# Recurrence of a two-layer encoder: diagonal blocks fetched by one DMA, level masks on VectorE, block inversion in one piece, four buffers of last decays

## What is computed

```python
def step(state, inp):
    r_t, w_t, k_t, v_t, kk_t, a_t = inp
    sk = jnp.einsum('bhij,bhj->bhi', state, kk_t)
    state = (state * w_t[:, :, None, :]
             - sk[..., None] * (kk_t * a_t)[:, :, None, :]
             + v_t[..., None] * k_t[:, :, None, :])
    y = jnp.einsum('bhij,bhj->bhi', state, r_t)
    return state, y
```

## Time and profile before

| | |
|---|---|
| median of 3 runs | 3150.53 us (3146.79 to 3151.83) |
| profiled execution: its own time | 3151.65 us |
| its span | 3149.8 us |
| busy PE / DVE / POOL / ACT | 86% / 54% / 41% / 30% of the span |
| recurrence, about 1627 to 2284 us | 657 us, a fifth of the span |
| in it PE / DVE / POOL / ACT busy | 431 / 432 / 257 / 150 us |
| mean granted clock of PE there | 0.84 |

### The profile page before, as it was taken

One profiled execution on the slowest core, in us unless ns is written; L12 is line 12 of the kernel. 1 busy time (PEld: TensorE's weight loads), 2 busy tenths in 40 slices (PEclk: granted clock), 3 DMA queues, 4 the chain that ended last, 5 costly groups with the idle time before them and its releaser, 6 DMA issues. The chain is left out here.

```text
span 3149.8 us, 48729 instructions
## 1 busy us (share of the span) xinstructions
PE 2694.7 (86%) x20064; PEld 2211.6 (70%) x20064; DVE 1692.8 (54%) x2038; ACT 930.1 (30%) x1543; POOL 1303.7 (41%) x662
## 2 busy tenths in 40 slices
PE   1887898999999999898965676777659999999999
PEld 1565676888877887776754566666647788878887
DVE  6745545665536344678635777777413543433444
ACT  2434433212233221545431222222124322222221
POOL 2532244444445343444433444444236444444443
PEclk9899998999999999999987988889879999999999
DMA  6421243545422232565752222222143233223333
GB/s 230 165 69 49 75 138 102 176 158 194 147 87 94 95 99 81 136 158 136 177 135 73 75 74 74 74 75 75 42 122 99 81 101 98 96 91 96 96 98 120
DMA packets 269146, 343.33 MB, mean 109 GB/s; under 512 B 180096, under 2 KB 180224, under 8 KB 268928
## 3 DMA queue, kind: packets, MB, share of 16 engines
q1 hardware_dynamic: 268928, 340.24, 35.8%
HBM read 298.29 MB, written 40.89 MB: 108 GB/s over the span
## 5 line engine op out<-in xcount | busy, mean ns | idle before, releaser
L687 POOL TENSOR_TENSOR wl<-w,wh 128x1024 fp32r<-128x1024 f32 x368 | 905.8, 2467 | 1308.5 <-ACT wh L728 1308.3
L180 PE MATMUL ps<-hi,wh 128*128 128x512 f32 x2208 | 883.1, 400 | 55.8 <-POOL wl L687 42.7
L181 PE MATMUL ps<-lo,wh 128*128 128x512 f32 x2208 | 868.9, 394 | 0.0
L182 PE MATMUL ps<-hi,wl 128*128 128x512 f32 x2208 | 868.8, 393 | 0.0
L728 ACT ACTIVATE wh<-w 128x1024 fp32r<-128x1024 f32 x368 | 388.1, 1057 | 717.6 <-DMA w<-in_ffn_w_in 529.7
L180 PEld LDWEIGHTS ps<-hi,wh 128*128 128x128 f32 x2208 | 420.3, 190 | 158.3 <-POOL wl L687 42.9
L994 DVE SCALAR_TENSOR_TENSOR xt<-ps,mod,xt 128x512 f32<-128x512 f32 x384 | 286.6, 750 | 438.3 <-PE ps L182 438.1
L181 PEld LDWEIGHTS ps<-lo,wh 128*128 128x128 f32 x2208 | 420.5, 190 | 89.9 <-issue 3.7
L182 PEld LDWEIGHTS ps<-hi,wl 128*128 128x128 f32 x2208 | 419.7, 190 | 90.1
L999 DVE TENSOR_TENSOR act<-ps,silu 128x512 f32<-128x512 f32 x88 | 60.8, 691 | 461.3 <-PE ps L182 461.3
L180 PE MATMUL ps<-act_hi,wh 128*128 128x512 f32 x704 | 282.8, 402 | 17.9 <-DVE act_lo L1003 10.9
(11 more groups left out here) (219 smaller groups left out, 3556.3 us busy)
## 6 DMA issues: line engine op xcount, KB each, us to landing
w<-in_ffn_w_in SPq DMA_DIRECT2D x176, 512.0 KB, 3.7
piece<-in_ada_w SPq DMA_DIRECT2D x96, 512.0 KB, 4.9
w<-in_ffn_w_out SPq DMA_DIRECT2D x88, 512.0 KB, 3.7
w<-in_w_rkv SPq DMA_DIRECT2D x48, 512.0 KB, 4.0
scratch<-silu SPq DMA_DIRECT2D x48, 256.0 KB, 3.1
scratch<-act SPq DMA_DIRECT2D x48, 256.0 KB, 3.0
w<-in_wqk SPq DMA_DIRECT2D x20, 512.0 KB, 4.6
xt<-in_xT SPq DMA_DIRECT2D x4, 2048.0 KB, 10.6
```

The lines of the kernel that those rows point to most:

```text
L180: pe.matmul(out, w_hi(k), x_hi(k), start=first and k == 0, stop=False)
L181: pe.matmul(out, w_hi(k), x_lo(k), start=False, stop=False)
L182: ins = pe.matmul(out, w_lo(k), x_hi(k), start=False, stop=last and k == kc - 1)
L687: pool.tensor_tensor(wl[n % NW][:, :, :], wr[n % NW][:, :, :], wh[n % NW][:, :, :].bitcast(F32), ALU.subtract).then_inc(*wlo.up)
```

## The change

Five edits, all in `wkv_phase`:

1. The images in memory are laid out by pair, half and row (each row of 64 numbers in a run of its own, 256 bytes), so that all 64 diagonal blocks can be addressed by one pattern. `n_diag` is read by one DMA instead of eight; `t_diag` and `t_diag_t` are written by one each instead of eight each. The transfers of whole images (N out, inverses in) keep their number; their runs become 256 bytes instead of 2 KB.
2. The two level masks are made by DVE from the gram in PSUM, right behind `n_t`, instead of by POOL from `n_t`. They now belong to x, no more to d.
3. `invert(d)` is one call behind `products_b(x)`, instead of three calls at the start of the period and around `level` and `products_k`.
4. `p_end` has four buffers, and `end_decay(x)` waits for the state of one period earlier.
5. Waits that go with these.

```diff
-                pend = [sb(f"p_end{b}", [P, PAIRS], c=c) for b in range(RING)]
+                pend = [sb(f"p_end{b}", [P, PAIRS], c=c) for b in range(RING + 1)]
...
+                def image(x, h):
+                    rows = x.rearrange("(a y) -> a y", a=PAIRS)[:, h * HEAD * (CHUNK + 1):h * HEAD * (CHUNK + 1) + HEAD * CHUNK]
+                    return rows.rearrange("a (p n) -> p a n", n=CHUNK)
+                def diagonal(x):
+                    rows = x.rearrange("(b y) -> b y", b=DP)[:, 0:BLK * CHUNK]
+                    return rows.rearrange("b (r n) -> b r n", n=CHUNK)[:, :, 0:BLK]
...
-                            for n in range(NX):
-                                h, n_h = divmod(n, NX // 2)
-                                sp.dma_start(nd[n * PAIRS:(n + 1) * PAIRS, 0:BLK * BLK].rearrange("p (r n) -> p r n", n=BLK),
-                                             diagonal(n_img[b, h], n_h)).then_inc(*nd_in.up)
+                            sp.dma_start(nd[:, :].rearrange("p (r n) -> p r n", n=BLK), diagonal(n_img[b])).then_inc(*nd_in.up)
...
+                            for w, x in enumerate((td, td_t)):
+                                sp.dma_start(diagonal(t_img[b, w]), x[:, 0:BLK * BLK].rearrange("p (r n) -> p r n", n=BLK)).then_inc(*t_out.up)
+                            sp.wait_ge(*t_out.at(2 * (ch + 1)))
...
-                            if d is not None:
-                                level_mask(d, 0), level_mask(d, 1)
...
-                            act.wait_ge(*g["s_done"].at(max(ch - 2, 0)))
+                            act.wait_ge(*g["s_done"].at(max(ch - 3, 0)))
...
                             masked(nt[ch % 2], 0, C_STRICT).then_inc(*g["nt_done"].up)
+                            dve.wait_ge(*g["x_done_w"].at(max(4 * ch - 4, 0)))
+                            for l in range(NL):
+                                masked(ntm[l][ch % 2], 0, C_LEVEL + (len(LEVELS) - NL + l) * CHUNK).then_inc(*g["lev_mask"].up)
                             dve.wait_ge(*g["chunk_used"].at(max(ch - 2, 0)))
...
                         def period(w, x, d, y, zz):
-                            if d is not None:
-                                invert(d, 1, 2)
                             if x is not None:
                                 bounded(x)
                             if y is not None:
                                 level(y, 0, 0), level(y, 0, 1)
                             if d is not None:
-                                products_k(d), invert(d, 4, 4)
+                                products_k(d)
                             if y is not None:
                                 level(y, 1, 0), level(y, 1, 1)
-                            if d is not None:
-                                invert(d, 8, 8)
                             if x is not None:
                                 decayed(x)
                             if zz is not None:
                                 centre(zz)
                             if x is not None:
                                 products_b(x)
+                            if d is not None:
+                                invert(d)
                             if zz is not None:
                                 new_state(zz)
```

More of the change, by code:

```diff
@@ L1372, in blocks_back @@
                                 for h in range(2):
-                                    sp.dma_start(x[b][h * HEAD:(h + 1) * HEAD, :, :], image(t_img[b, w, h])).then_inc(*t_in[b].up)
+                                    sp.dma_start(x[b][h * HEAD:(h + 1) * HEAD, :, :], image(t_img[b, w], h)).then_inc(*t_in[b].up)
                         for b in range(2):
@@ L1377, in _ @@
                                 for h in range(2):
-                                    sp.dma_start(image(t_img[b, w, h]), state[h * HEAD:(h + 1) * HEAD, :, :]).then_inc(*img_zero.up)
+                                    sp.dma_start(image(t_img[b, w], h), state[h * HEAD:(h + 1) * HEAD, :, :]).then_inc(*img_zero.up)
                         def period(w, x, d, y, zz):
@@ L1478, in end_decay @@
                             act.wait_ge(*g["e_done"].at(2 * ch + 2))
[L1479 to L1480 removed]
+                            act.wait_ge(*g["s_done"].at(max(ch - 3, 0)))
+                            act.activation(pend[ch % (RING + 1)][:, :].unsqueeze(2), ep[:, :, CHUNK - 1:CHUNK], ACT.Copy).then_inc(*g["pend_done"].up)
                         def values_out(ch):
@@ L1778, in small_product @@
                             step(dve.tensor_reduce(out, y, AX.X, ALU.add))
[L1780 to L1790, removed]
-                                for left, right, out in ((corner(td, 2, 2 * BLK + 1, 2, 1)[:, :, :, 0], corner(td, 2, BLK, 1, 1)[:, :, :, 0], corner(td, 2, 2 * BLK, 2, 1)[:, :, :, 0]),
-                                                         (corner(td, 2, 2 * BLK, 1, 2)[:, :, 0, :], corner(td, 2, 2 * DIAG + BLK, 1, 1)[:, :, 0, :], corner(td, 2, 3 * BLK, 1, 2)[:, :, 0, :])):
-                                    step(dve.tensor_tensor(x, left, right.to_broadcast([DP, count, 2]), ALU.mult))
-                                    step(dve.tensor_tensor(out, out, x, ALU.add))
-                                size = 4
-                            while size <= last:
@@ new lines, in invert @@
+                        def invert(ch):
+                            dve.wait_ge(*nd_in.at(ch + 1))
+                            dve.wait_ge(*t_out.at(2 * ch))
+                            step(dve.tensor_tensor(td[:, 0:BLK * BLK].rearrange("p (i j) -> p i j", j=BLK),
+                                                   nd[:, 0:BLK * BLK].rearrange("p (j i) -> p i j", i=BLK),
+                                                   eye[:, 0:BLK * BLK].rearrange("p (i j) -> p i j", j=BLK), ALU.add))
+                            count = BLK // 4
+                            x = tmp[:, 0:2 * count].rearrange("p (g i) -> p g i", i=2)
+                            for left, right, out in ((corner(td, 2, 2 * BLK + 1, 2, 1)[:, :, :, 0], corner(td, 2, BLK, 1, 1)[:, :, :, 0], corner(td, 2, 2 * BLK, 2, 1)[:, :, :, 0]),
+                                                     (corner(td, 2, 2 * BLK, 1, 2)[:, :, 0, :], corner(td, 2, 2 * DIAG + BLK, 1, 1)[:, :, 0, :], corner(td, 2, 3 * BLK, 1, 2)[:, :, 0, :])):
+                                step(dve.tensor_tensor(x, left, right.to_broadcast([DP, count, 2]), ALU.mult))
+                                step(dve.tensor_tensor(out, out, x, ALU.add))
+                            size = 4
+                            while size < BLK:
```

34 lines of the change are left out of this document (7 added, 27 removed).

## The result

The changed kernel takes 3192.04 us (median of 4 runs, 3189.52 to 3197.6) against 3151.18 us for the kernel before, run beside it (4 runs, 3146.79 to 3156.77). The ratio is 1.0131, with a 95% interval of 1.0109 to 1.0153: slower by 1.3%, some 41 us. The forecast was 3199 us, slower by 48, with a range of 3145 to 3250. The kernels of the experiments did not all run on the same chip as the changed kernel, so where two of them are compared, the difference of the ratios (0.01 is 31.5 us) is given beside the difference of the medians.

What follows compares the result with a forecast made beforehand. Bound: the recurrence's period of 37.06 us, pieces waiting for each other, with the detour through memory on the path. 27.8 + 3.0 + 9.9 = 40.7, +3.65 over 14 periods (+51), tail -3: 3199 us, range 3145 to 3250.

Steps and rivals of the forecast that it cites:

- Crux, steps 5 and 6: Inversion in one piece: 6.9 us, ending 27.8 us behind `kk` instead of 20.4; then the inverses' way out, about 3.0 us.
- Step 1: From `kk` to the level sums: `one_plus_x` about 5.7 us behind `kk`, held by PE's `x_st`; gain 4.2 us.
- Step 2: Between the two level sums: PE's pass now bare, 5.0 us (3.4 to 6.2) instead of 6.18.
- Step 3: DVE's `ar`, `ar`, `b_dec` beside POOL, each waiting for POOL's instruction: `b_dec` ends 16.0 us behind `kk`, before 22.2.
- Step 4: Gram: 2.3 us from `b_dec` to `n_t`; two masks cost nothing inside the wait for `r_b`, 20.3 us behind `kk`.
- Step 6: Inverses out by two DMAs instead of sixteen: about 3.0 us (2.2 to 4.5) for 7.0, gain 4.0.
- Step 7: First image read to next `kk`: 9.9 us (8.5 to 11) instead of 9.47, 0.4 added for 256-byte runs.
- Step 8: Four `p_end` buffers: needed, worth nothing alone; compute ready for `kk` at 33.4 us, so `kk` waits some 7 us for tile a.
- Rival B: Tiles are no limit at all, the period is compute's 33.4 us: 3100 us; chance 0.03.
- Tail: Behind the last periods no tiles are loaded and compute sets the pace: -3 us.
- A: Faster: PE keeps full clock, `b_dec` slips between POOL's instructions, inversion ends at 24.0; period 34.7, 3115 us; chance 0.15.
- C: Slower still: image runs and 64-byte writes land late, PE at low clock; period 44.5 us, 3250 us; chance 0.20.

## Why the prediction was right

The four stretches of which the sum was made, as means over the periods between 1800 and 2142 us (eight in the changed kernel), read from DVE's and SP's timelines:

| stretch | before | forecast | after |
|---|---|---|---|
| `kk` to the start of the inversion | 4.9 | 20.9 | 20.7 (19.8 to 21.7) |
| inversion to the first write | 16.1, with work between | 6.9 | 6.9 |
| first write to first image read | 7.3 | 3.0 | 3.8 (3.3, or 4.6 to 4.7) |
| first image read to `kk` | 9.4 | 9.9 | 9.5 |
| sum | 37.7 | 40.7 | 40.9 |

- Crux, steps 5 and 6: right. The inversion takes 6.9 us in one piece, and ends some 7 us later in the period than before (27.6 us behind `kk` in the mean, against 20.9). The wait at `kk` was given as 5 to 9 us, in the sum as 7; it is 4.2 to 6.3, in the mean 5.1, behind the first two periods with 10.6 each.
- Step 1, K to the first level sum: mis-sized. Forecast K+5.7, measured K+8.5 in the period shown; three of the eight periods have K+5.7, and the mean is K+7.0. I had taken `x_st` at K+5.8 from the earlier trace rows; in the period shown it comes at K+7.8, since PE idles through the wait at `kk` and starts norms and solution at clock 0.50. A wait that I forecast myself had a consequence that I did not follow to PE.
- Step 2: 4.0 us between the level sums against 5.0 (before 6.18). With step 1, the second sum stands at K+12.5 in the period shown, K+11.0 in the mean, instead of 10.7: two errors of about 1 us that offset each other, which is luck.
- Step 3: right, to the instruction. `ar` 1.36, `ar` 1.52, `b_dec` 0.68, against 0.68 without POOL: as the earlier trace rows had it. In the period shown `b_dec` ends at K+17.1, in the mean at K+15.5 (forecast 16.0; in the kernel before it ended at K+22.3, not 22.2).
- Step 4: the gram takes 2.1 us from `b_dec`'s end to `n_t` (forecast 2.3), and `r_b`, 1.9 us behind it, no longer waits. The masks stand in the place of that wait. On POOL's side step 3 had counted on their 2.46 us, but neither step gave them a price by itself; with the masks back on POOL the kernel was 14 to 21 us slower.
- Step 6: 3.3 us, in three of eight periods 4.6 to 4.7, against 3.0; the terms written there add up to 2.8. The two DMAs take 0.58 and 0.67 us to issue, more than the 0.4 in that sum.
- Step 7: 9.0 us with the old images and 9.5 with the new, against my +0.4. Single periods scatter from 8.2 to 9.8 and from 8.4 to 10.3, and the kernel before has 9.4 with the old images. So the runs don't decide between the earlier trace rows and the almost nothing that the 27% of the Trainium skill, "DMA: Bandwidth & Descriptors", section "Why small descriptors are slow (HBM only)", would have given.
- Step 8, four buffers: worth nothing, as said. But compute was mis-sized: not 33.4, in the period shown DVE was free for `kk` at K+36.5, and without the wait the period was 37.5. Step 8 took PE's work behind the state "as before", and did not follow that PE stands idle for 7.3 us ahead of it and then works at clock 0.50. The forecast didn't suffer, since the wait at `kk` covers it. Rival B, had it held, would have given 3133 and not 3100.
- Sum: +46.5 us over 14 periods, forecast +51. The other twelve periods took 41.0 us in the mean, as forecast; the first two took 36.7 and 36.4 us, while the pipeline filled, and I had priced all 14 alike. Tail: -2.7, forecast -3.

Of the rivals, A needed the inversion to end before K+25; it ended at K+27.6. C's late landings did not come. What the prediction did not see at all is what the parts are worth apart. In ratios to the kernel before, and in spans of the profiled execution:

| part | ratio to ratio | by the ratios, us | by the spans, us |
|---|---|---|---|
| new images | 1 to 0.9887 | -36 | -41 |
| masks on DVE, four buffers | 0.9887 to 0.9805 | -26 | -28 |
| inversion in one piece behind the gram | 0.9805 to 1.0131 | +103 | +114 |
| sum | 1 to 1.0131 | +41 | +46 |

The forecast set one net loss of 48 us, and the net is what came. But it is the difference of a move that costs over 100 us and two parts that give some 65, and I had given the masks no price of their own. The images I had at 4.0 less 0.4 us per period, 50 us in 14; alone they gave 36 to 41, in the changed kernel 51 to 60. Both numbers for the move hold only against the kernel with the other parts in it: there the wait for the tiles was no longer a limit, and the move made it one again. The experiments on the changed kernel split the move's 109 us by medians (3192 to 3083) further: 59 came back with the tiles ahead (54 by the ratios), 37 more with the state ahead too, and 13 stayed. What stays open is how much of the move's cost is PE's clock: the stage's mean falls from 0.90 to 0.80, and the tail is 12 us longer (971.3 against 958.8), but no run separated clock from queue there.

## What to carry to other kernels

Before a block of work is moved, name everything that stands in a queue behind its result, on every engine and on the DMA queue above all: here 5.6 us saved in the inversion lost to four loads that had nothing to do with it, and swapping two calls gave 54 to 59 us back. A wait in the profile may be cover for another wait on the same loop: follow the loop around once before pricing its removal. The wait for tile a in the kernel before went away and brought nothing, since the loads only changed their place in the loop; and with three buffers of last decays, which is what ACT's 124 us came of, the changed kernel was no slower. Where PE must pause in every period, look at the clock behind the pause; a few matmuls that compute nothing may pay for themselves.

## What was not expected of the hardware

- Behind an idle stretch of 4.8 us PE's next work ran at clock 0.50: the gram in 3.68 us instead of 1.96, and seven unused matmuls of 128x256 (3.3 us on an engine that was idle anyway) kept it at 1.00.
- A DMA of 64x16x16 floats took 0.58 or 0.67 us to issue, one of 8x16x16 0.33: eight times the runs of 64 bytes for twice the issue. From first write to first read, two of the large ones took 3.3 us in most periods and sixteen of the small ones 7.0, for the same bytes.
- The Trainium skill, "SBUF — State Buffer", section "SBUF: two separate sides", describes the port pair shared by DVE and GpSimd as an exclusive lock, held for the whole instruction. That agrees with `ar` in the changed kernel: the first ended within 0.6 us behind POOL's instruction beside it (1992.32 and 1991.77), and the second, started at 1992.24, behind POOL's next one (1993.76 and 1993.22), at twice its time alone. POOL's two instructions:

```profile
1990.48 1.29 POOL L1411 TENSOR_TENSOR rk<-r,k 128x512 f32<-128x512 f32 x1
1991.85 1.37 POOL L1413 TENSOR_TENSOR rk<-rk,vec 128x512 f32<-128x512 f32 x1
```
